# Output projections in one block: modulation sums beside the rounding, first pair of columns taken by chunks

## The reference, cut to what matters

```python
x = x + gate[:, None, :] * (y @ w_out[l])                  # first block, layers 0 and 1
xc = xc + gate_c * (yc @ w_out[l])                         # context rows, layer 0 alone
x = x + gate_m * (merged @ w_out[l])                       # second block
```

## Time and profile before

| | |
|---|---|
| median of 3 runs | 4788.84 us (4785.28 to 4797.52) |
| the profiled execution, its own time | 4786.71 us |
| its span, first to last instruction | 4784.9 us |
| TensorE busy with matmuls | 4007.2 us (84%) |
| VectorE, ScalarE, GpSimd busy | 2177.8, 1473.1, 905.0 us |
| mean granted TensorE clock over the span | 0.914 |

### The profile page before, as it was taken

One profiled execution on the slowest core, in us unless ns is written; L12 is line 12 of the kernel. 1 busy time (PEld: TensorE's weight loads), 2 busy tenths in 40 slices (PEclk: granted clock), 3 DMA queues, 4 the chain that ended last, 5 costly groups with the idle time before them and its releaser, 6 DMA issues. The chain is left out here.

```text
span 4784.9 us, 43684 instructions
## 1 busy us (share of the span) xinstructions
PE 4007.2 (84%) x16492; PEld 2896.3 (61%) x16492; DVE 2177.8 (46%) x2598; ACT 1473.1 (31%) x2342; POOL 905.0 (19%) x414
## 2 busy tenths in 40 slices
PE   6699779997689689998585989898999755999996
PEld 6578535556567445556363866576777644666664
DVE  0274356662355356641346623233442212666665
ACT  1211235551201144440214135412221011555552
POOL 0143210001143400003130102133333331111111
PEclk9899879997899889998798999999999985999998
DMA  4111101101211101212221212043343231999986
GB/s 156 60 36 32 34 15 31 31 27 49 80 44 38 42 27 53 64 60 99 30 31 53 49 33 26 11 72 75 80 97 70 63 136 52 345 350 352 353 293 224
DMA packets 354883, 450.97 MB, mean 94 GB/s; under 512 B 51997, under 2 KB 227314, under 8 KB 354178
## 3 DMA queue, kind: packets, MB, share of 16 engines
q1 hardware_dynamic: 342034, 423.12, 29.9%
q0 software_dynamic: 12656, 25.26, 1.5%
HBM read 408.41 MB, written 59.31 MB: 98 GB/s over the span
## 5 line engine op out<-in xcount | busy, mean ns | idle before, releaser
L1076 PE MATMUL values<-probs,vp 128*128 128x512 f32 x672 | 348.9, 601 | 12.0 <-issue 6.4
L1165 ACT ACTIVATE probs<-scores 128x512 f32<-128x512 f32 (+1 forms) x336 | 196.1, 584 | 309.2 <-PE scores L211 307.5
L1374 POOL TENSOR_TENSOR out_hi<-out_w,ones 128x1024 fp32r<-128x1024 f32 x24 | 57.3, 2387 | 1196.9 <-DMA out_w<-in_w_out 1196.9
L209 PE MATMUL scores<-q_hi,k_rest 97*128 97x512 f32 (+1 forms) x336 | 262.4, 781 | 0.0
L678 DVE SCALAR_TENSOR_TENSOR conv_out<-conv_in,vectors,conv_out 128x1295 f32<-128x1295 f32 (+1 forms) x120 | 254.2, 2118 | 4.3
L3258 PE MATMUL dp<-h_t,abt 128*128 128x512 f32 x544 | 241.9, 597 | 1.1 <-ACT abt L3307 0.9
L209 PE MATMUL out_ps<-h_t_r,out_w_r 128*128 128x512 f32 (+1 forms) x448 | 172.6, 385 | 68.0 <-POOL out_w_r L1376 68.0
L209 PE MATMUL gates_ps<-x_t_r,gates_w_r 128*128 128x512 f32 (+1 forms) x560 | 210.3, 375 | 21.9 <-POOL gates_w_r L259 21.9
L3289 ACT ACTIVATE expert_hi<-wu 128x1024 fp32r<-128x1024 f32 x136 | 144.9, 1065 | 252.1 <-PE gp L211 252.1
L1247 DVE TENSOR_REDUCE mx<-made 128x1 f32<-128x640 f32 (+1 forms) x272 | 203.8, 794 | 27.0 <-PE made L1017 26.4
L209 PE MATMUL smb<-x_t_r,merge_w_r 128*128 128x512 f32 x480 | 196.3, 409 | 19.3 <-POOL merge_w_r L2599 16.6
(11 more groups left out here) (523 smaller groups left out, 9872.9 us busy)
## 6 DMA issues: line engine op xcount, KB each, us to landing
wg<-in_w_gate SPq DMA_DIRECT2D x34, 2048.0 KB, 9.9
wu<-in_w_up SPq DMA_DIRECT2D x34, 2048.0 KB, 11.2
h_t<-in_w_down SPq DMA_DIRECT2D x34, 2048.0 KB, 9.8
ahead_w<-in_w_ada SPq DMA_DIRECT2D x48, 512.0 KB, 3.9
gates_w<-in_w_in SPq DMA_DIRECT2D x28, 512.0 KB, 3.9
mod_w<-in_w_mod SPq DMA_DIRECT2D x12, 1024.0 KB, 5.5
x_kept<-x_t SPq DMA_DIRECT2D x6, 2048.0 KB, 11.0
ahead_w<-in_w_mod SPq DMA_DIRECT2D x24, 512.0 KB, 3.5
```

The costliest lines, as they stand in the source:

```text
L209: nc.tensor.matmul(out, lhs[1], rhs[0], start=start, stop=False, **kw)
L1076: nc.tensor.matmul(O[b % 2][:, 0:w], vp[g // 2 % 2][:, kb, g % 2 * VD:g % 2 * VD + P], pr[m % 3][:, 0:w], start=kb == 0, stop=kb == nk - 1 ...
L1165: nc.scalar.activation(pr[m % 3][:, 0:w], S[m % 2][:, 0:w], ACT.Exp, scale=scale).then_inc(s.exped, 1)
L1374: nc.gpsimd.tensor_tensor(hi[:, c, :, :], wt[:, c, :, :], all_ones(k), ALU.mult).then_inc(s.split, 1)
```

## The change

The three stages become one, for each of the three projections.

- `finish_modulation` is gone. `attention` returns what it took, and `project_residual` gets it as `sums`. Its 48 matmuls come first in TensorE's program of the one stage, the two additions of the bias come on VectorE behind the rests. The load of the first residual waits for the sums, as they lie there.
- There is room for two pairs of weights (4 halves in place of 2). SyncE issues the loads of pairs 0 and 1 at the start of the stage; pairs 2 and 3 wait for the products of the pair two before.
- The first pair's weights are rounded on ScalarE, between chunks 0 to 3 and 4 to 7 of the values, and their rests are taken on VectorE at the same place of its order. GpSimd splits pairs 1 to 3, and begins when all 8 rests of the values are taken.
- TensorE takes pair 0 chunk by chunk: for each chunk the 3 passes of all tiles (6 in layer 0, 4 in the others), each in its own bank, as soon as that chunk's rest is there. The other pairs go as before.
- The `Fori` loops are written out.

```diff
-    finish_modulation(nc, k, acc, bias_next, chunks_next, conds, mod_next)
+    return acc, bias_next, chunks_next, conds, mod_next
...
-    with stage(nc, "rounded rest") as s, nc.Block() as block:
+    names = "w_in0 w_in1 w_in2 w_in3 x_in0 x_in1 x_in2 x_in3 rounded rest w_rounded w_rest split products added summed biased"
+
+    with ExitStack() as es, stage(nc, names) as s, nc.Block() as block:
+        wt, rest = es.enter_context(sbuf_views(nc, f"{name}_w", [P, 4, DK, P]))
+        hi = es.enter_context(sbuf(nc, f"{name}_hi", [P, 4, DK, P], F32R))
...
+        def place(g, c):
+            return 2 * (g % 2) + c
+
+        @block.sync
+        def _(sp):
+            for g in range(n_pairs):
+                for c in range(2):
+                    if g >= 2:
+                        sp.wait_ge(s.products, (g - 2) * per + (c + 1) * nb)
+                    sp.dma_start(wt[:, place(g, c), :, :], cols_of(w, 0, g)[:, :, c * P:(c + 1) * P])\
+                        .then_inc(w_in[place(g, c)], 16)
+                if g == 0:
+                    continue
+                if g == 1:
+                    if sums:
+                        sp.wait_ge(s.summed, 1)
+                    sp.dma_start(k.x[:, 0:2, first:T1], kept[:, 0:2, first:T1]).then_inc(x_in[0], 16)
+                pair = slice(2 * g, 2 * g + 2)
+                sp.dma_start(k.x[:, pair, first:T1], kept[:, pair, first:T1]).then_inc(x_in[g], 16)
+
+        @block.gpsimd
+        def _(pool):
+            pool.wait_ge(s.rest, DK)
+            for g in range(1, n_pairs):
...
+        @block.tensor
+        def _(pe):
+            if sums:
+                for n in range(conds * n_chunks):
+                    last = nc.tensor.matmul(sum_ps[:, n:n + 1], acc[:, n * P:(n + 1) * P], k.ones[:, 0:1],
+                                            start=True, stop=True)
+                last.then_inc(s.summed, 1)
...
+            pe.wait_ge(s.w_rest, 2)
+            for j in range(DK):
+                pe.wait_ge(s.rest, j + 1)
+                for t in range(per):
+                    m = product(0, t, j)
+                    if j == DK - 1:
+                        m.then_inc(s.products, 1)
+            for g in range(1, n_pairs):
+                for t in range(per):
+                    if t % nb == 0:
+                        pe.wait_ge(s.split, 4 * (g - 1) + 2 * (t // nb) + 2)
+                    pe.wait_ge(s.added, (g - 1) * per + t + 1)
+                    for j in range(DK):
+                        m = product(g, t, j)
+                    m.then_inc(s.products, 1)
+
         @block.scalar
         def _(act):
...
+            round_chunks(range(early))
+            for c in range(2):
+                act.wait_ge(w_in[c], 16)
+                nc.scalar.activation(hi[:, c, :, :], wt[:, c, :, :], ACT.Copy).then_inc(s.w_rounded, 1)
+            round_chunks(range(early, DK))
...
+            take_rests(range(early))
+            for c in range(2):
+                dve.wait_ge(s.w_rounded, c + 1)
+                nc.vector.tensor_tensor(rest[:, c, :, :], wt[:, c, :, :], hi[:, c, :, :].bitcast(F32), ALU.subtract)\
+                    .then_inc(s.w_rest, 1)
+            take_rests(range(early, DK))
+            if sums:
+                dve.wait_ge(s.summed, 1)
+                for i in range(2):
+                    at = min(i, conds - 1) * n_chunks
+                    nc.vector.tensor_tensor(mod_next[:, :, i], sum_ps[:, at:at + n_chunks], k.vec[:, tile, row:row + n_chunks],
+                                            ALU.add).then_inc(s.biased, 1)
```

More of the change, by code:

```diff
@@ L384 @@
 AHEAD = D
-def finish_modulation(nc, k, acc, bias, n_chunks, conds, dst):
-    tile, row = k.at[bias]
-    with stage(nc, "summed biased") as s, nc.Block() as block, psum(nc, "ahead_ps", [P, 512], F32) as ps:
-        @block.tensor
-        def _(pe):
-            for n in range(conds * n_chunks):
-                last = nc.tensor.matmul(ps[:, n:n + 1], acc[:, n * P:(n + 1) * P], k.ones[:, 0:1], start=True, stop=True)
-            last.then_inc(s.summed, 1)
-        @block.vector
-        def _(dve):
-            dve.wait_ge(s.summed, 1)
-            for i in range(2):
-                at = min(i, conds - 1) * n_chunks
-                nc.vector.tensor_tensor(dst[:, :, i], ps[:, at:at + n_chunks], k.vec[:, tile, row:row + n_chunks],
-                                        ALU.add).then_inc(s.biased, 1)
 def norm_factors(nc, k, dst, norm, mod, scale_at, n):
@@ new lines, in take_rests @@
+            def take_rests(chunks):
+                for j in chunks:
+                    dve.wait_ge(s.rounded, j + 1)
+                    nc.vector.tensor_tensor(src_r[:, j, :], src[:, j, :], k.h_r[:, j, 0:total].bitcast(F32),
+                                            ALU.subtract).then_inc(s.rest, 1)
+            take_rests(range(early))
+            for c in range(2):
+                dve.wait_ge(s.w_rounded, c + 1)
+                nc.vector.tensor_tensor(rest[:, c, :, :], wt[:, c, :, :], hi[:, c, :, :].bitcast(F32), ALU.subtract)\
+                    .then_inc(s.w_rest, 1)
@@ new lines, in _ @@
+            take_rests(range(early, DK))
+            if sums:
+                dve.wait_ge(s.summed, 1)
[3 more added lines that the diff above has]
+                                            ALU.add).then_inc(s.biased, 1)
+            for g in range(n_pairs):
+                dve.wait_ge(x_in[g], 16)
+                for t in range(per):
+                    c, b = divmod(t, nb)
+                    t0, w_, which = blocks[b]
+                    dve.wait_ge(s.products, g * per + t + 1)
+                    n = 2 * g + c
+                    x = k.x[:, n, t0:t0 + w_]
+                    nc.vector.scalar_tensor_tensor(x, ps[t][:, 0:w_], mod[:, gate_at + n, which:which + 1], x,
+                                                   ALU.mult, ALU.add).then_inc(s.added, 1)
@@ L1440, in first_layer @@
         conv.close()
-        attention(nc, k, a, l, last, cq, ckv, kr, ahead)
+        sums = attention(nc, k, a, l, last, cq, ckv, kr, ahead)
     project_residual(nc, k, f"out{l}", a.w_out[l], k.y[:, :, blocks[0][0]:T1], k.y_r[:, :, blocks[0][0]:T1],
-                     blocks, mod, 2 * DK, k.kept)
+                     blocks, mod, 2 * DK, k.kept, sums)
 I32 = mybir.dt.int32
```

89 lines of the change are left out of this document (24 added, 65 removed).

## The result

The changed kernel took 4749.58 us, median of 4 runs (4747.09 to 4753.27), against 4790.70 us (4785.28 to 4797.52, 4 runs) of the kernel before beside it: a ratio of 0.9914 with a 95% interval of 0.9897 to 0.9931. It is faster by 41 us. 4732 was forecast with a range up to 4747, so the time is 18 us above the forecast and 2.6 us outside the range.

What follows compares the result with a forecast made beforehand. TensorE was taken as the bound, busy 84% of the span, with idle stretches before each projection's first product to win. 23.4 + 21.3 + 12.2 = 56.9 us less gave 4732 us (0.988), own range 4722 to 4741, 8-in-10 range 4720 to 4747.

Steps and rivals of the forecast that it cites:

- Part 1: Layers 0 and 1: preparation hides beside the sums, so the first product follows the last sum; 23.4 and 21.3 us less.
- part 2: Second block's projection, without sums: earlier preparation brings the first product near 3765.5 in place of 3777.70, 12.2 us less.
- stretched: Rival, layers 0 and 1: other engines' work and loads beside the sums lengthen them, up to 4 us; no separate chance.
- rival of late weights: Second block: loads share the queue's rate, weights come late and nothing is gained there; 4744 us, chance 0.07.
- The clock: Products' start in each projection: low-clock time unchanged, 0; rival of pair 0 at the low clock, 4784 us, chance 0.03.
- the banks: Pair 0 by chunks: bank changes after every three matmuls cost 0; rival that each is paid, 19 us, 4751, chance 0.06.
- the ramps: First products of the three projections: TensorE's low-clock stretches of 5.3, 5.9 and 5.7 us stay unchanged, term 0.
- ramps of 5 to 6 us: Sign that the forecast is right: TensorE's low-clock start of products still lasts 5 to 6 us in the projections.
- the bound of 8.4: Most that could be won in the three projections if products had no low-clock start at all: 8.4 us.
- Written-out loops cost nothing that I can see: Projections' loops written out: cost taken as 0, since the loop's first pass is straight code and had no hole.
- so nothing gives the gain back: Stages after the projections: each starts anew behind a barrier and only begins earlier, so none of the 56.9 us is lost.
- cut by something unseen: Place unnamed: an unseen cause reduces the gain, which still stays over 0.3%; chance 0.03.

Runs made afterwards that it cites:

- after_tile_order: The changed kernel with pair 0 taken tile by tile once all 8 rests are there: 4758.78 us, ratio 0.9929 to the kernel before.
- after_again: The changed kernel once more with nothing changed, for a second profile: 4750.91 us, ratio 0.9914 to the kernel before.
- before_pe_written_out: The kernel before with TensorE's loop alone in the output projections written out: 4804.20 us, ratio 1.0033.
- only_second_block: The kernel before with the change in the second block's projection alone: 4781.71 us, ratio 0.9973.

## Why the prediction was off

**Right.** Part 1 and part 2 hold term by term: 23.6, 21.2 and 12.1 us up to the first product, where 23.4, 21.3 and 12.2 were forecast. The sums took 20.61 and 19.19 us beside the other engines' work, 20.61 and 18.96 before: stretched by 0.2 us at most. The preparation was done 5.6 us ahead of their end (5.7 forecast). In the second block the weights landed at 3735.17 - 3730.81 = 4.4 and some 6.2 us after SyncE's first issue (4.1 and 5.6 forecast), and the first product came 8.52 us behind ScalarE's first rounding (8.4 forecast): the rival of late weights did not come. Once begun, TensorE has no hole.

**The clock and the banks.** Both were taken as 0. For the banks that holds. Pair 0 runs at 1.00 with a bank change every three matmuls, starts 0.23 us apart within a bank (1120.89, 1121.12, 1121.35) and 0.24 us across (1122.40, 1122.64). The one change that the prediction had read, 1148.19 to 1148.40, still lay in the ramp at 0.50, so it told nothing of changes at 1.00. after_tile_order, without these changes, gained 1.3 and 0.1 us more in layers 0 and 1, no more than two profiles of one kernel differ in layer 1 (22.5 and 20.1); in layer 0 its clock also reached 1.00 after 3.0 us of products, not 5.1, which is some 1 us of the 1.3. The Trainium skill, "TensorE: Matmul & The Clock Gate", section "A second HAM failure mode: psum-queue depth-cycling", tells of a kernel whose clock swung under such an order; this case's trace doesn't agree.

For the ramps it holds in layer 0 alone, 5.1 us for 5.3. In layer 1 and the second block the clock was at 1.00 after 3.0 and 2.9 us of products, where 5.9 and 5.8 had been, so the sign "ramps of 5 to 6 us" failed there. From the first product to the last it is 88.3 and 91.2 us for 89.7 and 92.5: 2.7 us gained, within the bound of 8.4, and most of why the projections gained 60.1 and not 56.9 us. In after_again these ramps are 5.2 and 3.5 us, so in layer 1 it is chance.

**Wrong.** The step that failed: "Written-out loops cost nothing that I can see", with "so nothing gives the gain back". The term was set to 0 for a reason that holds only inside the projection: straight code has no hole there, and before_pe_written_out shows that too. Its cost lies elsewhere, for the most part in stages behind both projections of the first block. It measured 1.0033, 15.8 us (9.6 to 22), in before_pe_written_out. With it the sum closes within what is known: the projections of the changed kernel gained 24.2 + 22.5 + 13.4 = 60.1 us in one profile and 57.5 in the other; less 15.8 that is 44.3 or 41.7 us, and 4790.7 less that 4746.4 or 4749.0, beside 4749.58 measured. The range failed with it, for no rival had a cost outside the three projections: each was a mechanism of the stage that the change edits, and "cut by something unseen" had a chance of 0.03.

**What is shown of the cause, and what is not.** Shown: writing out TensorE's loop alone costs the kernel before the 0.33%. Shown too: a longer TensorE program, and nothing else tried, changes which of the second block's loads of 512-byte rows land late, and the "ssm" stage gets some 12 to 14 us longer; a short program in the changed kernel takes that away. This comes back in all 20 kernels of the table, with only_second_block in between. That the late loads are what TensorE waits for is read from its waits, 6.5 and 10.0 us longer; no run changes the loads alone. Not shown: that length alone makes the whole kernel lose 15 us. With waits in place of written out code the medians show 1 us, and with the change in the first block alone 3. Not shown either: how a program's length does that. The one candidate tried, an unused tensor in DRAM, changed nothing. It is also not understood why packets took less time each (35 for 45 ns) while a whole load took as long. The "merge" stage gives 11 us of the 24 back, and that isn't explained either.

## What to carry to other kernels

Line up the two traces stage by stage over the whole kernel, not only where the edit is: a term can be right to 0.2 us and the sum wrong by 15, in a stage that nobody edited. That a loop's body has no hole doesn't make writing the loop out free; keep the loop and test it alone against the code written out. Where an order or a second buffer only serves a stretch that is covered already, leave it out: by tiles in layers 0 and 1 with TensorE's loop kept was the best kernel measured here, 0.9883.

## What the runs showed of the hardware that was not expected

- A TensorE program 617 instructions longer (14851 for 14234) changed the loads of stages far away: 512-byte packets took 35 ns on average for 45, and the two stages got 9.7 and 12.7 us longer. A program made longer with waits did the same to the packets and the "ssm" stage (35.5 ns, 5.6 and 11.8 us longer), but the kernel lost next to nothing by it outside the waits. GpSimd's program 1000 waits longer did nothing.
- The mean packet time says little of how a load serves: at 35 and at 45 ns a packet the twelve loads of the "ssm" stage took 104.5 and 103.0 us in sum. Which of the twelve were late differed, the same way in every kernel of a kind.
- 96 records of one-column matmuls keep TensorE busy for 20.48 of 20.70 us and the granted clock stays at 0.50, 1.2 GHz, as it did before. In layer 1 the clock was at 1.00 some 3 us into the products, in after_again 5.2, and 5.1 in layer 0.
- A float32 matmul of two columns against ones took as long as one of one column: 10.37 us for 48 records, 20.61 for 96.
